# Two norms of a two-block transformer on one Trainium2 core: the last squares summed by the tensor engine, and an earlier split of one weight unit

## What is computed

```python
merged = gates[0] * y_pool + gates[1] * y_sb + gates[2] * y_x
h = h + rmsnorm(merged @ w_out[l], norm_mix_post[l])      # first place
n2 = rmsnorm(h, norm_ffn_pre[l])
gu = n2 @ w_ffn_in[l]
ff = (jax.nn.silu(gu[..., :D_FF]) * gu[..., D_FF:]) @ w_ffn_out[l]
h = h + rmsnorm(ff, norm_ffn_post[l])                     # second place
h = _rmsnorm(x, norm_mix[layer])                          # second block
q, f, i, g = jnp.split(h @ w_in, 4, axis=-1)              # the recurrence's inputs
```

## Time and profile before

| | us |
|---|---|
| median of 3 runs | 2015.29 |
| their range | 2014.92 to 2015.47 |
| the profiled execution's own time | 2015.5 |
| its span, first to last instruction | 2013.7 |

### The profile page before, as it was taken

How to read it: one execution, slowest core, us unless ns; L and a number is a source line. 1 busy time by engine, 2 the same in 40 slices (tenths; PEclk the granted TensorE clock), 3 DMA queues, 4 the chain that set the end, 5 groups by cost and what they waited for, 6 DMA issues and landing times.

```text
span 2013.7 us, 26586 instructions
## 1 busy us (share of the span) xinstructions
PE 1993.1 (99%) x10917; PEld 1621.0 (80%) x10917; DVE 975.9 (48%) x1511; ACT 940.9 (47%) x1322; POOL 860.7 (43%) x670
## 2 busy tenths in 40 slices
PE   9999999999999999999999999999999999999999
PEld 7788888878888887677777888888877788888887
DVE  6644443254201315898984553255157645522551
ACT  6666663353223225666664543244267645432441
POOL 2344334526544543443334544444431255444443
PEclk9999999999999999999999999999999999999999
DMA  6122222223232221121212223222210222322231
GB/s 259 53 94 74 74 74 94 95 74 105 95 104 94 94 99 58 64 74 64 75 64 94 94 98 102 88 101 97 86 48 27 79 94 95 101 98 92 97 102 66
DMA packets 51817, 178.31 MB, mean 89 GB/s; under 512 B 5744, under 2 KB 8944, under 8 KB 51568
## 3 DMA queue, kind: packets, MB, share of 16 engines
q1 hardware_dynamic: 51696, 176.61, 26.0%
HBM read 174.49 MB, written 2.10 MB: 88 GB/s over the span
## 4 chain that ended last, share of the span: by engine, by line
PE 92%; DVE 5%; ACT 2%; issue 1%; DMA 0%; POOL 0%; SPq 0%; ACTq 0%; DVEq 0%; POOLq 0%
PE ps_gemm L228 24%; PE ps_gemm L230 24%; PE ps_gemm L229 24%; PE ps_attend L228 4%; PE ps_attend L230 4%; PE ps_attend L229 4%; PE ps_attend L912 1%; PE ps_attend L1777 1%; PE ps_attend L2620 1%; PE ps_attend L2687 1%; PE ps_attend L2622 0%; PE ps_attend L925 0%; PE ps_attend L2621 0%; PE ps_attend L285 0%; ACT weights_high L203 0%
## 5 line engine op out<-in xcount | busy, mean ns | idle before, releaser
L2900 POOL TENSOR_TENSOR weights_low<-weights_raw,weights_high 128x512 fp32r<-128x512 f32 (+1 forms) x331 | 433.0, 1308 | 1108.0 <-ACT weights_high L203 1107.8
L228 PE MATMUL ps_gemm<-normed_high,weights_high 128*128 128x512 f32 x1665 | 658.3, 395 | 3.9 <-DVE normed_low L1322 3.3
L230 PE MATMUL ps_gemm<-normed_low,weights_high 128*128 128x512 f32 x1665 | 646.9, 389 | 0.0
L229 PE MATMUL ps_gemm<-normed_high,weights_low 128*128 128x512 f32 x1665 | 646.4, 388 | 0.0
L203 ACT ACTIVATE weights_high<-weights_raw 128x1024 fp32r<-128x1024 f32 (+1 forms) x340 | 339.4, 1006 | 447.0 <-PE ps_attend L230 215.6
L2901 POOL TENSOR_TENSOR weights_low<-weights_raw,weights_high 128x512 fp32r<-128x512 f32 (+1 forms) x331 | 437.8, 1323 | 0.0
L228 PEld LDWEIGHTS ps_gemm<-normed_high,weights_high 128*128 128x128 f32 x1665 | 312.6, 188 | 74.3 <-DVE normed_low L1322 5.0
L230 PEld LDWEIGHTS ps_gemm<-normed_low,weights_high 128*128 128x128 f32 x1665 | 312.6, 188 | 65.0
L229 PEld LDWEIGHTS ps_gemm<-normed_high,weights_low 128*128 128x128 f32 x1665 | 312.8, 188 | 63.5 <-issue 1.9
L228 PE MATMUL ps_gemm<-operands_high_low,weights_high 128*128 128x512 f32 (+1 forms) x552 | 216.1, 392 | 0.8 <-ACT weights_high L203 0.3
L230 PE MATMUL ps_gemm<-operands_high_low,weights_high 128*128 128x512 f32 (+1 forms) x552 | 214.1, 388 | 0.0
(11 more groups left out here) (340 smaller groups left out, 2179.1 us busy)
## 6 DMA issues: line engine op xcount, KB each, us to landing
weights_raw<-weights_full SPq DMA_DIRECT2D x317, 512.0 KB, 3.2
weights_raw<-weights_short SPq DMA_DIRECT2D x24, 128.0 KB, 2.0
residual<-x_tiles SPq DMA_DIRECT2D x4, 512.0 KB, 7.5
out_tiles<-residual SPq DMA_DIRECT2D x8, 256.0 KB, 2.1
parameters<-params SPq DMA_DIRECT2D x1, 1559.5 KB, 10.4
scratch<-memory_tiles SPq DMA_DIRECT2D x2, 256.0 KB, 4.9
scratch<-memory_tiles SPq DMA_DIRECT2D x1, 512.0 KB, 5.8
scratch<-positions SPq DMA_DIRECT2D x1, 256.0 KB, 10.6
```

Source lines behind the costliest of these rows:

```text
L228: t.op.matmul(out, m.wh[:, c:c + P], xh, start=start and n == 0, stop=False, skip_group_check=True)
L229: t.op.matmul(out, m.wl[:, c:c + P], xh, start=False, stop=False, skip_group_check=True)
L230: ins = t.op.matmul(out, m.wh[:, c:c + P], xl, start=False, stop=stop and n == len(pairs) - 1, skip_group_check=True)
L2900: g.op.tensor_tensor(m.wl[:, a], m.raw[:, a], m.wh[:, a].bitcast(F32), ALU.subtract)
```

## The change

In words: `dve_half_sum` is gone. `pe_half_total` sends to PE not one matmul on the finished sum but several that add up in one PSUM bank: one on the sum that DVE has so far, and one on each square that DVE did not add. At the first place that is the square of tile 7 alone (`first_alone` is 7), at the second the squares of tiles 6 and 7 (it is 6). The useless matmuls ahead of and between the totals of the second place are gone, and one of three behind them. Tile 7 of the feed-forward output is kept in scratch. The rounding of the recurrence's third weight unit stands behind the square of tile 4 in ACT's program.

```diff
--- before.py
+++ after.py
@@ -1207,28 +1207,41 @@
     return tokens(m.gb(2) if half else m.gb(0), (half,))
 
 
+def first_alone(stage):
+
+    return KD - 1 if stage == "mixed" else KD - 2
+
+
+def last_squares(m):
+    return m.sq_tile(1)
+
+
 def pe_half_total(m, t, stage, half):
-    t.wait_ge(*m.V.at(stage, "sum", KD - 1, half))
-    pe_sum_over_partitions(m, t, (stage, "total", half), half_total(m, stage, half), tokens(m.ss[:, :], (half,)))
+
+    out, ones, first = half_total(m, stage, half), m.col("ones", 0, P), first_alone(stage)
+    t.wait_ge(*m.V.at(stage, "sum", first - 1))
+    t.op.matmul(out, ones, tokens(m.ss[:, :], (half,)), start=True, stop=False, skip_group_check=True)
+    for j in range(first, KD):
+        if j < KD - 1:
+            t.wait_ge(*m.A.at(stage, "square", j))
+            src = m.sq_tile(j % 2)
+        else:
+            t.wait_ge(*m.A.at(stage, "square", j, half))
+            src = last_squares(m)
+        ins = t.op.matmul(out, ones, tokens(src, (half,)), start=False, stop=j == KD - 1, skip_group_check=True)
+    ins.then_inc(*m.T.mark(stage, "total", half))
 
 
 def act_half_square(m, s, stage, half, src):
     if half == 0:
         s.wait_ge(*m.V.at(stage, "sum", KD - 3))
-    s.op.activation(tokens(m.sq_tile(1), (half,)), src, ACT.Square).then_inc(*m.A.mark(stage, "square", KD - 1, half))
+    s.op.activation(tokens(last_squares(m), (half,)), src, ACT.Square).then_inc(*m.A.mark(stage, "square", KD - 1, half))
 
 
 def act_half_rstd(m, s, stage, half):
     s.tables(LOGEXP)
     s.wait_ge(*m.T.at(stage, "total", half))
     act_rstd(m, s, (stage, "rstd", half), tokens(m.rstd2, (half,)), half_total(m, stage, half), D)
-
-
-def dve_half_sum(m, v, stage, half):
-    out = tokens(m.ss[:, :], (half,))
-    v.wait_ge(*m.A.at(stage, "square", KD - 1, half))
-    v.wait_ge(*m.V.at(stage, "sum", KD - 2))
-    v.op.tensor_tensor(out, out, tokens(m.sq_tile(1), (half,)), ALU.add).then_inc(*m.V.mark(stage, "sum", KD - 1, half))
 
 
 def act_project_mix(m, s):
@@ -1254,14 +1267,12 @@
 def dve_project_mix(m, v):
     for j in range(KD - 1):
         dve_square_sum(m, v, "mixed", j)
-    dve_half_sum(m, v, "mixed", 0)
     dve_branch(m, v, "mixed", "ffn0", 0, (0,), "g_mix_post")
-    dve_half_sum(m, v, "mixed", 1)
 
 
 def branch_tile(m, stage, j):
 
-    return m.bank(j) if stage == "hgrn" and j >= WIDE else m.big_tile(j)
+    return m.bank(j) if stage == "hgrn" and WIDE <= j < KD - 1 else m.big_tile(j)
 
 
 def act_post_norm(m, s, before, stage, gain):
@@ -1513,12 +1524,12 @@
             elif n == 0 and j < KD - 1:
                 s.wait_ge(*m.V.at(stage, "kept", g, j))
                 act_square(m, s, stage + "out", j, branch_tile(m, "hgrn", j))
+                if j == 4:
+                    high_to(m, s, fourth_unit(m, "hgrn") - 1)
             elif n == 0:
                 for half in range(2):
                     s.wait_ge(*m.V.at(stage, "kept", g, j, half))
-                    act_half_square(m, s, stage + "out", half, tokens(m.bank(j), (half,)))
-                    if half == 0:
-                        high_to(m, s, fourth_unit(m, "hgrn") - 1)
+                    act_half_square(m, s, stage + "out", half, tokens(m.big_tile(j), (half,)))
             elif n == 1 and g:
                 h, hi, _ = residual_tile(m, j)
                 s.wait_ge(*m.V.at("mla", "residual", j))
@@ -1587,22 +1598,16 @@
 
     f, ps = m.big_tile(KD - 1), m.bank(KD - 1)
     for half in range(2):
-        out = tokens(ps, (half,))
-        v.op.tensor_tensor(out, tokens(f, (half,)), out, ALU.add).then_inc(*m.V.mark("ffn0", "kept", 1, KD - 1, half))
-        if half == 0:
-            dve_square_sum(m, v, "ffn0out", KD - 2)
-            dve_half_sum(m, v, "ffn0out", 0)
-    dve_half_sum(m, v, "ffn0out", 1)
+        out = tokens(f, (half,))
+        v.op.tensor_tensor(out, out, tokens(ps, (half,)), ALU.add).then_inc(*m.V.mark("ffn0", "kept", 1, KD - 1, half))
     dve_unit_low(m, v, fourth_unit(m, "hgrn") - 1)
 
 
 def pe_post_ffn(m, t):
-    t.wait_ge(*m.V.at("ffn0", "kept", 1, 1))
-    pe_keep_busy(m, t, m.gb(1), (512, 256))
+    t.wait_ge(*m.V.at("ffn0", "kept", 1, 2))
     pe_half_total(m, t, "ffn0out", 0)
-    pe_keep_busy(m, t, m.gb(1), (128,))
     pe_half_total(m, t, "ffn0out", 1)
-    pe_keep_busy(m, t, m.gb(1), (512, 512, 256))
+    pe_keep_busy(m, t, m.gb(1), (512, 512))
 
 
 def dve_residual(m, v, stage, j, ps, out, gain):
```

## The result

The changed kernel takes 2018.21 us (median of 22 executions, 2017.77 to 2020.19), the kernel before 2015.72 us (22 executions, 2014.92 to 2016.76). The ratio is 1.0014, with a 95% interval from 1.0008 to 1.002: slower by 2.5 us in the medians. That is within the 0.2% that were called no change, and outside the forecast range, which ended at 2018.0. The forecast was added to 2015.29, the median of three runs of the kernel before; over 22 that median is 0.43 us higher. Taken as differences, the forecast was +1.0 us with a range up to +2.7, and +2.49 was measured: so the median lies beyond the range only by the level from which the forecast started, and the size of the change was still off by 1.5 us.

A forecast was written before the change was run, and what follows sets the result against it. PE, busy 99% of the span, was taken to bound the kernel. First place +0.15 and second place +0.87 us made +1.0 us on 2015.3, so 2016.3 us; own range 2015.5 to 2017.1, 8-in-10 range 2014.5 to 2018.0.

The forecast's parts named there:

- What bounds the kernel: Whole kernel: a stream of PE matmuls, PE busy 99%; changes count only where PE stands still or does unneeded work.
- First place: At 415 to 425 us: an extra total matmul shifts ACT's logarithm +0.38 us, DVE's piece of half 1 comes +0.15 us later.
- Second place, the rounding: At 782 to 792 us: ACT waits at the rounding until 781.57, squares of tiles 5 and 6 follow; +0.87 us.
- Rival 1: Second place: the early rounding works and squares come as today; -0.8 us there, 2014.65 us in all; chance 0.13.
- Second place, tile 7: Second place: keeping tile 7 in scratch instead of PSUM costs nothing that can be seen.
- The ladder: Both places: the step-by-step timing of a dozen handoffs, giving +1.0 us and 2016.3 us; chance 0.75.
- rival 2: Second place: the clock falls in PE's new 1.7 us gap ahead of the totals; 5.7 us, 2021.0 us; chance 0.05.
- The removed matmuls: Second place: useless matmuls behind the totals, 256 columns fewer, end at about 788.2 and neither delay nor matter.
- The weaker form of the rival: Second place: the clock falls behind the totals instead of ahead of them; 2018.4 us.
- Rival 3: Both places: shifts cancel through unseen DVE slack; first wins up to 0.2 us, second loses about 0.7; 2015.8 us; chance 0.07.

The follow-up runs named there:

- e3: Changed kernel with the rounding of the third weight unit back behind the square of tile 7's half 0; 2016.66 us.
- e6: Kernel before with only the rounding of the third weight unit moved behind the square of tile 4; 2017.35 us.
- e2: Kernel before with only tile 7 of the feed-forward output kept in scratch; 2017.49 us.
- e12: e10 without the useless matmuls behind the totals of the second place; 2015.13 us.
- e7: Changed kernel with tile 7's product with gain and factor written to the free PSUM bank, so only the residual add reads one operand from PSUM; 2017.10 us.
- e8: e7 with the rounding of the third weight unit also at its old place; 2015.18 us.
- e1: Changed kernel with tile 7 kept in its PSUM bank again, ACT squaring both halves only after both are kept; 2017.18 us.
- e4: Kernel before with only the first place changed, two total matmuls per half instead of DVE's half sum; 2015.80 us.
- e5: Changed kernel with the edits of e1 and e3 together: tile 7 in its PSUM bank and the rounding at its old place; 2015.38 us.
- e9: Changed kernel with useless matmuls of 512 and 256 columns back ahead of the second place's totals; 2018.16 us.
- e10: Changed kernel with the rounding at its old place, tile 7's half 0 in scratch and later copied by DVE into its PSUM bank, half 1 in the bank; 2015.06 us.
- e11: e10 with the first place as in the kernel before, with its half sums; 2015.04 us.

## Why the prediction was wrong, point by point

**What bounds the kernel** was right: the change of time lies at the two places and in what DVE and POOL do behind them, and PE gave nothing back.

**First place.** Forecast +0.15 us, measured +0.03 (A), and +0.01 with this place alone. The step was mis-sized: the extra total matmul delayed ACT's logarithm not by 0.38 but by about 0.28 us (415.07 in the changed kernel, less the 0.47 us by which this execution is late there, against 414.32), and the 0.17 us to spare plus the overlap of neighbours covered it. PE waited only 0.77 us for the piece at 420.20, not 1.04, because its own first piece had come later by as much.

**Second place, the rounding.** Right. The wait on the slot's old unit held ACT for 2.13 us, the squares of tiles 5 and 6 followed, and B grew by 0.93 us where +0.87 was forecast. e3 and e6 confirm it from both sides. Rival 1, in which the early rounding works, is refuted by that wait; e3, where no rounding stands ahead of the squares, shows what it would have been worth, -0.77 us in B (forecast -0.8).

**Second place, tile 7.** This is the step that failed: "Tile 7 in scratch instead of PSUM costs nothing that I can see." It cost 1.54 us (C), and e2 gives it alone as 1.56. The prediction put it at nothing without naming a row, and did not look at what POOL runs when that tile is used, some 16 us after it is written. With that term the sum is 0.03 + 0.93 + 1.54 = 2.50 us. The ladder's own range ended at 2017.1, and the wider one at 2018.0, just short of rival 2; neither had room for a term left out. The term left out is larger than all that was forecast.

**The removed matmuls.** Of those behind the totals the prediction said that "they neither delay nor matter"; that holds for the medians, in e12 too. Those ahead of the totals were the matter of rival 2. It had a chance of 0.05 as an event of the whole kernel; by the reading of e7's profile it came true in 4 of 22 executions, at a cost of 1.6 to 2.1 us, less than half of the 4.7 us that I had worked out: in e7's profile the clock was back at full in the stretch from 788 us on. The median does not show it. The weaker form of the rival, a fall behind the totals, was priced at 2.1 us; in e12's profiled execution it cost 0.47. One piece of the evidence against the rival was read wrongly: the gap of 1.45 us at the very start stands ahead of the very matmuls that I priced as slow, 5.10 us where 3.0 is the full rate, so it says nothing for a full clock. That evidence went no further than the 1.27 us of the earlier trace rows.

**Rival 3** (the shifts cancel) named the half sum of 1.18 us as its clue and expected a gain from it. That row was the collision with POOL in small.

## What to carry to other kernels

Before an operand moves from PSUM to SBUF, look at what GpSimd runs when that operand is used, not only when it is written: a DVE operation that then reads two tiles in SBUF can more than double (0.69 to 1.67 us here), and slows GpSimd as well. Before an instruction moves ahead in an in-order program, read the condition it waits for and find when that comes true; idle time at the new place is not enough. And matmuls that do nothing may be holding the clock: remove them only where the gap they fill has gone too, and look at all executions, not the median alone.

## What was not expected of the hardware

Two things. First, the collision of DVE and POOL costs both: 1.0 us for one DVE add of 0.69 us, 0.8 us for POOL's two operations of 1.3 us, and where the DVE operation starts first, as the multiply of 0.76 us in e8, only POOL pays for it. Second, whether the clock falls is not the same from one execution of a program to the next. With PE's gap of 1.83 us ahead of the totals (changed kernel, e1, e7) 8 of 44 executions granted less than 1.000 and were over a microsecond longer than the median of their run's executions at 1.000; with the gap of 1.90 us in e6, and with that of 2.43 us in e12, 7 of 11 granted less. At the first place the pair of totals brings it, alone in e4 (3 of 11): the seven runs with the new first place and without the open gap ahead of the totals (e3, e4, e5, e8, e9, e10, e12) have granted less than 1.000 in 19 of 77 executions, 7 of them in e12, whereas the kernel before, e2 and e11, with the old first place, have none in 120. (e6 has the old first place too; its profiled execution lost clock at the second, behind its gap.) In e10's profiled execution the clock was at 0.60 in 420 to 422 us and at 0.54 in the 2 us behind, and A was 15.95 us as ever: where DVE sets the pace, a half clock on PE cost nothing. What it is in the new order that lets the clock fall there was not tried.
